# Attention probabilities divided by their sums on GpSimd before the transposes, and latent-attention scores computed in partition groups

## The reference

```python
q_a, k_a, v_a, z_a, c_q, c_kv, k_rope, z_b = jnp.split(proj, idx, axis=-1)
o_a = dilated_window_attention(q_a, k_a, v_a, rel_bias)      # A: 8 heads of 64; softmax of scores + bias
...
q_nope = rmsnorm(q[..., :64], qn_gain)                       # B: 8 heads, from latent c_q and c_kv
q_rope = rope(rmsnorm(q[..., 64:], qr_gain), cos, sin)
k_nope = rmsnorm(kv[..., :64], kn_gain)                      # kv = rmsnorm(c_kv) @ w_ukv, per head: 64 keys, 64 values
k_rope = rope(rmsnorm(k_rope_in, kr_gain), cos, sin)         # one for all heads
s = (einsum('bqhd,bkhd->bhqk', qn, k_nope) + einsum('bqhd,bkd->bhqk', qr, k_rope)) * scale
s = jnp.where(qpos >= kpos, s, -inf)                         # causal
p = jax.nn.softmax(s, axis=-1)
o_b = einsum('bhqk,bkhd->bqhd', p, v)
...
mixed = jnp.concatenate([o_a * silu(z_a), o_b * silu(z_b)], axis=-1)
out = jnp.matmul(mixed, w_out)
```

## Time and profile before

| | before |
|---|---|
| three runs | 2492.61, 2495.91, 2496.38 us |
| median | 2495.91 us |
| the profiled execution | 2493.65 us, span 2491.9 us |
| PE busy | 2407.6 us, 97% |
| PE weight loads | 1905.8 us, 76% |
| VectorE busy | 1111.3 us, 45% |
| ScalarE busy | 712.4 us, 29% |
| GpSimd busy | 1031.6 us, 41% |
| mean granted PE clock | 0.991 of full speed |

### The profile page before, as it was taken

The page is one execution under the profiler, slowest core; times in us unless marked ns, Lnnn a source line. Parts: engine busy times, 40 slices in busy tenths (PEclk is TensorE's granted clock), DMA queues, the critical chain, the costliest instruction groups (busy, mean ns, idle before and its releaser), DMA issues.

```text
span 2491.9 us, 35573 instructions
## 1 busy us (share of the span) xinstructions
PE 2407.6 (97%) x15294; PEld 1905.8 (76%) x15294; DVE 1111.3 (45%) x1360; ACT 712.4 (29%) x1096; POOL 1031.6 (41%) x684
## 2 busy tenths in 40 slices
PE   7999999999999989999999999999999999989999
PEld 6888777777778868878888887888677866646677
DVE  4240113223185354677676674335333226665521
ACT  3101122222232121244344341103222015564411
POOL 4323323323223378577777763345622210122221
PEclk9999999999999999999999999999999999999999
DMA  5111322222200146422223224221213111001014
GB/s 194 52 43 50 94 82 71 85 68 85 68 26 4 46 153 202 135 80 85 81 77 93 85 94 176 102 101 43 51 35 109 51 59 39 1 9 27 1 60 127
DMA packets 208309, 189.77 MB, mean 76 GB/s; under 512 B 16778, under 2 KB 186993, under 8 KB 207898
## 3 DMA queue, kind: packets, MB, share of 16 engines
q1 hardware_dynamic: 208154, 187.51, 24.2%
HBM read 141.31 MB, written 45.13 MB: 75 GB/s over the span
## 4 chain that ended last, share of the span: by engine, by line
PE 88%; DVE 7%; ACT 2%; POOL 2%; issue 1%; DMA 0%; SPq 0%; DVEq 0%; POOLq 0%; ACTq 0%
PE gp L1135 14%; PE gp L1137 13%; PE gp L1136 13%; PE sm L1620 3%; PE sm L1621 3%; PE sm L1622 3%; PE gp L1620 3%; PE gp L1621 3%; PE gp L1622 3%; PE sm L1820 2%; PE gp L1722 2%; PE gp L1738 2%; PE gp L1649 2%; PE sm L1650 2%; PE sm L1649 2%; PE sm L1651 2%
## 5 line engine op out<-in xcount | busy, mean ns | idle before, releaser
L1135 PE MATMUL gp<-h_hi,w_hi 128*128 128x512 f32 x1264 | 507.2, 401 | 1.3 <-ACT k_sb L1925 1.3
L1137 PE MATMUL gp<-h_hi,w_lo 128*128 128x512 f32 x1264 | 492.8, 390 | 0.0
L1136 PE MATMUL gp<-h_lo,w_hi 128*128 128x512 f32 x1264 | 492.4, 390 | 0.0
L882 POOL CAST w_hi<-w_raw 128x1024 fp32r<-128x1024 f32 (+1 forms) x121 | 130.5, 1079 | 809.0 <-PE gp L1137 537.2
L884 POOL TENSOR_TENSOR w_lo<-w_raw,w_hi 128x1024 fp32r<-128x1024 f32 (+1 forms) x129 | 342.4, 2655 | 10.3 <-ACT w_hi L2053 0.5
L1135 PEld LDWEIGHTS gp<-h_hi,w_hi 128*128 128x128 f32 x1264 | 237.3, 188 | 70.8 <-issue 23.7
L1136 PEld LDWEIGHTS gp<-h_lo,w_hi 128*128 128x128 f32 x1264 | 237.5, 188 | 51.1 <-issue 4.3
L1137 PEld LDWEIGHTS gp<-h_hi,w_lo 128*128 128x128 f32 x1264 | 237.3, 188 | 50.9
L2449 DVE TENSOR_TENSOR_SCAN sb_run<-sb_keep,ones_row 128x128 f32<-128x128 f32 (+7 forms) x32 | 77.1, 2449 | 318.0 <-POOL sb_keep L929 318.0
L1050 POOL TENSOR_TENSOR w_lo<-w_sum,w_hi 128x512 fp32r<-128x512 f32 x66 | 96.3, 1460 | 45.8 <-ACT w_hi L2112 45.8
L2273 ACT ACTIVATE att_s<-att_s,small 128x1024 f32<-128x1024 f32 (+7 forms) x128 | 98.7, 773 | 9.4 <-DVE small L2921 8.7
(11 more groups left out here) (528 smaller groups left out, 5198.4 us busy)
## 6 DMA issues: line engine op xcount, KB each, us to landing
w_raw<-in_w_in SPq DMA_DIRECT2D x79, 512.0 KB, 4.3
gates_spill<-gate_out SPq DMA_DIRECT2D x32, 512.0 KB, 3.1
gate_in<-gates_spill SPq DMA_DIRECT2D x30, 512.0 KB, 4.3
w_raw<-in_w_up SPq DMA_DIRECT2D x22, 512.0 KB, 4.9
up_raw<-in_w_up SPq DMA_DIRECT2D x22, 512.0 KB, 5.0
g_spill<-hid SPq DMA_DIRECT2D x22, 512.0 KB, 2.6
g_stage<-g_spill SPq DMA_DIRECT2D x22, 512.0 KB, 4.3
w_raw<-in_w_down SPq DMA_DIRECT2D x22, 512.0 KB, 3.6
```

What stands on the lines that cost most here:

```text
L882: pool.tensor_copy(w_hi[:, t % 2, 0:n], w_raw[:, t % 2, 0:n]).then_inc(s["w_high"], 1)
L1135: pe.matmul(o, wh, hi[:, k0 + k, c], start=(k == 0), stop=False)
L1136: pe.matmul(o, wh, lo[:, low[k] if low else k0 + k, c], start=False, stop=False)
L1137: mm = pe.matmul(o, wl, hi[:, k0 + k, c], start=False, stop=(k == n - 1))
```

## The change

**Division.** GpSimd gets a function `even(u)`: once VectorE has written the reciprocals of unit u (`at_root`), it multiplies the unit's two rows of exponentials in `att_s` by them, in place, one `tensor_scalar` per head over the unit's width. PE's `turn(u)` waits for these (`at_even`) and no longer for ScalarE's exponentials (`at_p`). The two matmuls of `output(u)` (L1732) and VectorE's second product (L2956) are gone.

**Scores of B.** A unit's width is cut in halves. Four matmuls of 64 rows (two halves by two heads, L1824 of the changed kernel) take the normalised rows; four of 32 rows (L1830) add the rotated ones in PSUM, each in another quarter of the partitions: the first half of the columns from `q_rope`, the second from `q_swap`, a copy of it with its partition halves exchanged. Two transfers per pair of tiles make that copy in place of the four that filled `q_tile`. `q_tile` is one tile of normalised rows per pair of heads, the rotated keys are read from `k_rope` where they lie, and GpSimd's copies and zeroings are gone. VectorE normalises a pair in one operation of 128 partitions (L2997 of the changed kernel).

**GpSimd's order.** The splits of the last weight tiles and of the gate rows are put between the calls of `even`.

```diff
+            def even(u):
+                pool.wait_ge(s["at_root"], u + 1)
+                w = P * (at_unit(u)[1] + 1)
+                for hh in range(2):
+                    row = att_s[:, at_place(u), hh, 0:w]
+                    pool.tensor_scalar(row, row, at_small(2, u, hh), None, ALU.mult).then_inc(s["at_even"], 1)
+
+            for u in range(UNITS):
+                even(u)
+                if u in (12, 15):
+                    split_weights(T_UKV + (u - 12) // 3)
...
-            def k_roped(hh, rows):
-                pool.tensor_copy(k_tile[rows, :, hh, :],
-                                 k_rope[rows, :].unsqueeze(1).to_broadcast([32, 4, T])).then_inc(s["tiles"], 1)
...
-            split_weights(T_OUT)
-            split_weights(T_OUT + 1)
-            for j in range(4):
-                pool.wait_ge(s["at_o_taken"], UNITS + NB * (j + 1))
-                split_mix(2 * j)
-                split_mix(2 * j + 1)
+            for u in range(UNITS, 2 * UNITS):
+                even(u)
+                if u % NB == NB - 1:
...
+                        split_weights(T_OUT)
+                        split_weights(T_OUT + 1)
+                if u % NB == 2 and u > UNITS + NB:
+                    j = (u - UNITS) // NB - 1
+                    pool.wait_ge(s["at_o_taken"], UNITS + NB * (j + 1))
+                    split_mix(2 * j)
+                    split_mix(2 * j + 1)
+            pool.wait_ge(s["at_o_taken"], 2 * UNITS)
+            for n in range(6, 8):
+                split_mix(n)
...
                 def turn(u):
-                    pe.wait_ge(s["at_p"], 2 * (u + 1))
+                    pe.wait_ge(s["at_even"], 2 * (u + 1))
...
-                    pe.wait_ge(s["at_root"], u + 1)
-                    for hh in range(2):
-                        pe.matmul(at_share_place()[C * hh:C * hh + C, :], at_small(2, u, hh).to_broadcast([P, C]),
-                                  ident[:, :], start=True, stop=True, skip_group_check=True)
...
+                for n in range(2):
+                    for hh in range(2):
+                        rows = slice(C * hh, C * hh + C)
+                        pe.matmul(place(hh, n), q_tile[j][rows, q], k_tile[rows, j, 0, m * n:m * n + m],
+                                  start=True, stop=False, skip_group_check=True)
+                for n in range(2):
+                    for hh in range(2):
+                        g = (2 * (j % 2) + hh + 2 * n) % 4
+                        rows = slice(32 * g, 32 * g + 32)
+                        mm = pe.matmul(place(hh, n), (q_rope[j // 2][:, :], q_swap[j // 2])[n][rows, q],
+                                       k_rope[rows, m * n:m * n + m], start=False, stop=True, skip_group_check=True)
+                        if n:
+                            mm.then_inc(s["at_z"], 1)
...
-                    dve.tensor_tensor(z, z, at_o_place()[:, ::step], ALU.mult).then_inc(s["at_half_gated"], 1)
-                    dve.wait_ge(s["at_half_gated"], u + 1)
-                    dve.tensor_tensor(z, z, at_share_place()[:, ::step], ALU.mult).then_inc(s["at_o_taken"], 1)
+                    dve.tensor_tensor(z, z, at_o_place()[:, ::step], ALU.mult).then_inc(s["at_o_taken"], 1)
...
-                for hh in range(2):
-                    rows = slice(C * hh, C * hh + C)
-                    ins = dve.scalar_tensor_tensor(tile[rows, hh, :], raw[rows, :], gain[rows, :],
-                                                   hrt[rows, i % 2, :], ALU.mult, ALU.mult)
-                ins.then_inc(s["n2_q"], 1)
+                gain = pcol("kn") if kind == "k" else q_scaled[:, 0:1]
+                dve.scalar_tensor_tensor(raw, raw, gain, hrt[:, i % 2, :], ALU.mult, ALU.mult).then_inc(s["n2_q"], 1)
```

More of the change, by code:

```diff
@@ L1705, in z @@
                         pe.wait_ge(s["at_s"], 2 * u)
[L1706 to L1713 removed]
+                    scores(*at_unit(u))
                 def turn(u):
[L1716 removed]
+                    pe.wait_ge(s["at_even"], 2 * (u + 1))
                     for c, r in at_chunks(u):
```

83 lines of the change are left out of this document (31 added, 52 removed).

## The result

The changed kernel takes 2538.47 us (median of four runs, 2535.53 to 2540.7) against 2495.31 us of before in the same comparison. The ratio is 1.017 with a 95% interval of 1.0152 to 1.0188. The forecast was 2480, with a range of 2466 to 2512. The measured time lies outside it, on the side of the first rival (GpSimd becomes the bound, 2522 us, chance 0.19), beyond that rival's figure and just beyond its range (2499 to 2535).

What follows compares the result with a forecast made beforehand. TensorE, busy 97% of the span, was taken as the bound. A -5.6, B -7.2, GpSimd's splits +1.2, latent products -3.2 and B's start -0.3 summed to -15.1 us: 2480 us forecast, range 2466 to 2512.

Steps and rivals of the forecast that it cites:

- first rival: GpSimd's products at 2.8 ns a column become the bound, place 3 (896 columns) late in B: 2522 us, chance 0.19.
- GpSimd takes the division: GpSimd's two products per unit: 1.04 to 1.3 us each at 1024 columns, hidden; splits queuing behind them add 1.2 us.
- hidden case: GpSimd's division is covered by existing waits, so the forecast's total of -15.1 us stands; chance 0.62, 2466 to 2489.
- the sum: Whole kernel: the terms for both attentions, GpSimd's splits, latent products and B's start total -15.1 us, 2480.8 against the median.
- Shares and rounds: Both attentions: two share matmuls (0.22 us a unit) and VectorE's second product go; rounds 30.0 us in A, 35.5 in B.
- Scores of B: Second attention's scores in 64-row and 32-row blocks: 1.15 us at width 128, 3.07 at 1024.
- second rival: B's 32-row score matmuls do not run four at once: +13 us, 2493, no change; chance 0.08.
- third rival: No drain between B's two score blocks: 0.2 us less a unit, 2475; counted inside the likeliest case.
- Regrouping: B's scores in row groups, by themselves: -0.35 us a round, gain at width 1024 given back at 128.
- Latent products: Stage between the attentions: one VectorE normalising operation of 128 partitions in place of two of 64, -3.2 us.
- Starts: First turns of the attentions, now behind VectorE's reciprocals and GpSimd's products: +1.1 us in A, -0.3 net in B.
- Splits in the queue: GpSimd's weight and mix splits beside its products: covered up to about 1.6 us, +0.4 us a round, +1.2 in all.

Runs made afterwards that it cites:

- run of forms: Changed kernel with another form of GpSimd's operation in each round (product by column or constant, broadcast product, copy, sum, minimum); 2523.82 us in one run.
- e1: Changed kernel with each GpSimd product cut to the first 128 columns of its row, the rest left undivided; 2482.78 us.
- e3: Changed kernel without the division on GpSimd: share matmuls and VectorE's second product back, the other parts kept; 2489.41 us.
- e13: Changed kernel with the division left out altogether, turns waiting for ScalarE's exponentials as before; 2478.35 us.
- e2: Changed kernel with each GpSimd product cut to the first half of its row, the second half left undivided; 2489.65 us.
- e12: Changed kernel with 4 to 10 dummy matmuls on TensorE ahead of turns with long waits for GpSimd; 2535.74 us.

## Why the prediction was wrong

**The step that failed** is the price under "GpSimd takes the division": "I take 1.04 to 1.3: a one-input operation should cost as one." Measured are 2.84 us at 1024 columns and 2.50 ns a column. The forecast had the right bound before it: read with all its excess in the columns, the row of L915 gives 2.8 ns a column and 3.0 us. It was one row against many. But those many were copies and casts, and the one was the only row of the operation that the change adds. The trace of before also had float32 products and sums in plenty, all with two inputs but for L915, and none of 1024 columns below 2.36 us. One of these groups:

```profile
L1002 POOL TENSOR_TENSOR merged<-merged,gated 128x1024 f32<-128x1024 f32 x24 | 64.8, 2700 | 19.0 <-DVE gated L2638 16.6
```

A product with one input costs about as much as this one with two. The run of forms shows that they are different prices, 1.04 us for a copy and 2.76 to 2.84 for any one-input arithmetic tried. The sentence of the Trainium skill (GPSIMD Engine Reference, § 4.1, "1-input is roughly line-rate") does not hold here for such products. A copy takes 1.04 us for 1024 columns, and the product 2.7 times as much.

**The rival had the mechanism.** It said that at 2.8 ns a column GpSimd becomes the bound, and gave 2522 us. Its figure for A was +27 over the hidden case, and the trace has +25.8 from the first turn to the last output, against e1. Some of that agreement is luck, since 5.2 us of it are TensorE at the lower clock, for which the rival had no term; the waits alone came to 20.6. Its figure for B was +15, and measured are +29.2. The widest unit was rightly sized: its turn now waits 2.3 us in three rounds, but the 1.25 us of waiting for VectorE inside the turn are gone for it in the last two of them, so that it ends 1.1 us late there, as the rival said (2.2 in the second round). The rest was too small or missing:
- Place 3 starts 3.2, 4.7 and 4.7 us late (from place 2's start, against e1), not 3.6 each: 12.7 us in place of 10.8.
- The turns and scores of place 3 behind these waits run at the lower clock and take 6.5 us more than in e1. There was no term for that.
- B's second round starts with a wait of 2.6 us, behind the two weight splits that follow the first round's products, and its last unit waits 1.5 us. The rival had weight splits in A only.

**The rest of the sum held.** With the product made cheap (e1), the time is 2482.78 us against the 2480.8 that the sum gives. Against its own before, e1 is 12.0 us faster, where the sum has 15.1 and would have 16.3 without its 1.2 for the splits; the starts make the difference.
- *Shares and rounds:* A's rounds were forecast at 30.0, and the second and third are 30.03. B's were forecast at 35.5 and are 35.43 and 35.53.
- *Scores of B:* the forecast's 1.15 us at width 128 contain 0.09 for leaving the full layout, which in the trace lies in the turn ahead. Without it they are 1.06 and 2.98 at 1024, and the changed kernel's blocks take 0.97 and 2.99. The four groups of 32 rows run side by side (four starts within 0.02 us), so the second rival falls. Between the two blocks a start comes 0.25 us behind the last one, where two starts in the middle of the 64-row block lie 0.16 apart, so the drain is there and the third rival falls too.
- *Regrouping:* forecast at 0.35 us a round. e3 shows 0.11. That the rest lies under waits is likely, but was not tested.
- *Latent products:* forecast -3.2 us; -3.1 to -3.4 in the experiments and -2.0 in the changed kernel's profiled execution.
- *Starts:* the second miss. Forecast were +1.1 in A and -0.3 in B; e1 has +2.3 and +3.3. The hop over GpSimd costs 2.5 and 2.4 us there (e13 against e1): the first turn used to run ahead of the reciprocals. B's start is 1 us longer than before without any hop too (e13); its cause was not looked for.
- *Splits in the queue:* "covered up to about 1.6 us" was right for products alone. It was wrong with splits behind them: 1.56 us costs 6.9 us more than 0.60 (e2 against e1), nearly all of it in rounds with splits. The forecast's +0.4 a round was too low from there on.

The time as a function of the price at 1024 columns is then 2482.8 us at 0.60 (e1, where every unit's product takes this), 2489.7 at 1.56, 2493.1 at 1.89, and 2538.5 at 2.84. It bends where a round's products and splits no longer fit beside TensorE's work.

Open is how much of B's 29 us the clock costs in the end. TensorE is busy 9.8 us longer there, but with quicker turns TensorE waits longer for GpSimd elsewhere (place 3 of e12's second round starts 8.1 us behind place 2, in place of 6.9), and in e12 the low stretches moved instead of going away.

## What to carry to other kernels

When a trace has one row of the very operation that a change adds and many rows of its relatives, price the change by the one row, or measure a form of it before anything is built on it; on GpSimd a copy says nothing about a product. Work that moves to an idle engine is hidden only up to the slack at each single place: look for what else stands in that engine's queue there, and count the waits it makes on TensorE with the clock behind them. And when a change has several parts, each may have the other sign: here two of them were worth 5 us, and the third took 49 back.

## What the runs showed of the hardware

- GpSimd in float32, at 128 partitions and 1024 columns: copy 1.04 us, one-input product, sum or minimum with a scalar 2.76 (constant) to 2.84 (column), product with a broadcast second operand 1.89. At 128 columns these are 0.29, 0.53 to 0.60, and 0.40. A product of two full tiles of 1024 columns takes 2.70 (L1002 before).
- VectorE's SBUF to SBUF product of 256 columns took 2.50 us while GpSimd ran a subtraction, 0.81 beside a cast, and 0.35 otherwise. Its copies out of PSUM did not suffer: 690 ns each in the changed kernel, with GpSimd busy for four fifths of the time, and 686 in before. The Trainium skill, Advanced Engine Details and Errata, VectorE Performance Modes, says that VectorE's faster mode between SBUF and SBUF uses a port that it shares with GpSimd, and that the two block each other there. With that rule the trace agrees, for the products and for the copies.
- Four 32-row matmuls in four partition groups run at once. For a unit of 384 columns (192 a half) the block of four takes 0.53 us (2360.24 to 2360.77), and the block of four 64-row ones ahead of it 0.85 (2359.39 to 2360.24). Between two starts in the middle of the 64-row block lie 0.16 us. With four such steps in one block and two in the other, 0.21 us is left over in each.
- TensorE's granted clock fell to 0.50 within an idle stretch of 4.75 us in B and stayed there for 4.9 us of the work behind it. Behind a wait of 3.28 us in A it was low twice and 1.00 once; behind one of 2.32 us in B it was 1.00 in the changed kernel and 0.52 in e12.
